# Three-pass fp32r products for values, queries and keys in a streaming attention, convolution and expert layer

## The reference, cut to what matters

```python
z = xn @ w_in                      # [c_q 512 | c_kv 512 | k_rope 64 | B 1024 | C 1024 | h 1024]
q = (rmsnorm(c_q, g_q) @ w_uq).reshape(B, T, N_HEADS, QK_NOPE + ROPE_DIM)   # 8 heads, 128 + 64
q_nope = q[..., :QK_NOPE]
q_rope = rope(q[..., QK_NOPE:], pos)
c_kv = rmsnorm(c_kv, g_kv)
k_rope = rope(k_r[:, :, None, :], pos)[:, :, 0, :]
q_lat = jnp.einsum('bthn,lhn->bthl', q_nope, w_uk)
...
o_lat = mla_attend(q_lat, q_rope, keys_ckv, keys_kr, pos, k_pos)
attn = jnp.einsum('bthl,lhv->bthv', o_lat, w_uv).reshape(B, T, ATTN_W)
...
conv_out = gate_b * conv           # short causal convolution over C * h
y = jnp.concatenate([rmsnorm(attn, g_ao), rmsnorm(conv_out, g_co)], axis=-1) @ w_o
```

## Time and profile before

| | |
|---|---|
| median of 3 runs | 1520.82 us (1520.22 to 1526.09) |
| the profiled execution's own time | 1520.34 us |
| its span, first to last instruction | 1518.4 us |
| TensorE busy, weight loads aside | 1343.2 us (88%) |
| VectorE busy | 590.5 us (39%) |
| ScalarE busy | 347.6 us (23%) |
| values, pairs of heads | 271 to 307 us, 307 to 419 us of the span |

### The profile page before, as it was taken

One profiled execution on the slowest core, in us unless ns is written; L12 is line 12 of the kernel. 1 busy time (PEld: TensorE's weight loads), 2 busy tenths in 40 slices (PEclk: granted clock), 3 DMA queues, 4 the chain that ended last, 5 costly groups with the idle time before them and its releaser, 6 DMA issues.

```text
span 1518.4 us, 22122 instructions
## 1 busy us (share of the span) xinstructions
PE 1343.2 (88%) x8510; PEld 714.2 (47%) x8511; DVE 590.5 (39%) x1175; ACT 347.6 (23%) x595; POOL 32.4 (2%) x41
## 2 busy tenths in 40 slices
PE   6999999999999999787888888888889988888885
PEld 4989999566666663232222222322323322232221
DVE  4335444044574443242243234224324422332344
ACT  5332322123453322111111111111212111111113
POOL 1000000000000000000000000000000000000000
PEclk9999999999999989999898888988989989898887
DMA  9454451023353368999999999999989999999994
GB/s 324 131 166 137 161 167 61 10 70 111 92 180 112 131 285 355 408 432 430 432 433 432 429 433 433 431 429 433 433 369 400 432 434 432 428 434 432 432 428 180
DMA packets 69751, 473.91 MB, mean 312 GB/s; under 512 B 9532, under 2 KB 46656, under 8 KB 55824
## 3 DMA queue, kind: packets, MB, share of 16 engines
q1 hardware_dynamic: 68640, 470.78, 76.0%
q0 software_dynamic: 832, 2.48, 0.4%
q10 hardware_dynamic: 240, 0.09, 0.0%
HBM read 469.97 MB, written 3.38 MB: 312 GB/s over the span
## 4 chain that ended last, share of the span: by engine, by line
PE 52%; DMA 41%; DVE 3%; issue 2%; ACT 1%; DVEq 0%; SPq 0%; ACTq 0%
DMA ring<-in_w_down 41%; PE ps L888 11%; PE ps L587 5%; PE ps L588 5%; PE ps L589 5%; PE ps L873 3%; PE ps L649 2%; PE ps L676 2%; PE ps L739 2%; PE ps L740 2%; PE ps L741 2%; PE ps L752 2%; PE ps L850 2%; PE ps L670 1%; PE ps L879 1%
## 5 line engine op out<-in xcount | busy, mean ns | idle before, releaser
L1566 DVE TENSOR_TENSOR hreg<-ps,hreg 128x512 f32<-128x512 f32 (+1 forms) x396 | 239.4, 677 | 291.6 <-PE ps L899 291.6
L873 PE MATMUL ps<-ring,mix 128*32 128x512 f32 x2112 | 278.4, 675 | 31.7 <-DMA ring<-in_w_up 19.5
L888 PE MATMUL ps<-ring,mix 128*32 128x512 f32 x1056 | 165.7, 784 | 62.5 <-DMA ring<-in_w_down 54.7
L899 PE MATMUL ps<-mix 32*128 32x512 f32 (+1 forms) x792 | 156.3, 612 | 26.4 <-ACT mix L1249 25.6
L1206 ACT COPY mix<-ps 128x512 f32<-128x512 f32 x66 | 70.5, 1068 | 446.4 <-PE ps L873 446.4
L873 PEld LDWEIGHTS ps<-ring,mix 128*32 128x32 f32 x2112 | 74.5, 121 | 206.3 <-issue 176.2
L587 PE MATMUL ps<-xT_hi,w_hi 128*128 128x320 f32 (+1 forms) x528 | 165.6, 314 | 2.9 <-DVE w_lo L1301 2.9
L588 PE MATMUL ps<-xT_lo,w_hi 128*128 128x320 f32 (+1 forms) x528 | 164.6, 312 | 0.0
L589 PE MATMUL ps<-xT_hi,w_lo 128*128 128x320 f32 (+1 forms) x528 | 164.5, 312 | 0.0
L1301 DVE TENSOR_TENSOR w_lo<-ring,w_hi 128x1024 fp32r<-128x1024 f32 (+1 forms) x66 | 76.8, 1204 | 110.5 <-ACT w_hi L1019 110.5
L888 PEld LDWEIGHTS ps<-ring,mix 128*32 128x32 f32 x1056 | 39.6, 138 | 162.7 <-issue 104.4
(11 more groups left out here) (258 smaller groups left out, 1186.5 us busy)
## 6 DMA issues: line engine op xcount, KB each, us to landing
ring<-in_w_gate SPq DMA_DIRECT2D x31, 4096.0 KB, 22.2
ring<-in_w_up SPq DMA_DIRECT2D x31, 4096.0 KB, 23.7
ring<-in_w_down SPq DMA_DIRECT2D x31, 4096.0 KB, 23.7
ring<-in_w_in SPq DMA_DIRECT2D x32, 1024.0 KB, 8.2
ring<-in_w_o SPq DMA_DIRECT2D x16, 1024.0 KB, 6.7
ring<-in_w_up SPq DMA_DIRECT2D x2, 2048.0 KB, 11.7
ring<-in_w_gate SPq DMA_DIRECT2D x2, 2048.0 KB, 8.4
ring<-in_w_down SPq DMA_DIRECT2D x2, 2048.0 KB, 22.3
```

Of the source, the lines that this page charges most:

```text
L873: last = pe.matmul(ps[r:r + B, bank, :], x[:, k % 4, k // 4, :], w[:, k, :], start=k < 4, stop=k >= KC - 4)
L888: last = pe.matmul(ps[B * j:B * (j + 1), 4, :], h[:, c, :], w[:, c, 512 * j:512 * j + 512], start=c == 0, stop=c == 3)
L899: pe.matmul(ps[0:tn, COMB_BANKS[u % 8], :], gates[r, t0:t0 + tn], rows[r, :], start=True, stop=True).then_inc(full_sem, 1)
L1566: dve.tensor_tensor(h, ps[0:tn, COMB_BANKS[u % 8], :], h, ALU.add).then_inc(signal, 1)
```

## The change

The products of values, queries and keys are each formed in three fp32r passes from high and low parts. ScalarE casts each operand to fp32r, VectorE subtracts the cast from the original. The operands are the four chunks of `wv` (128x1024 each), of `ckv` (128x576 each), `cq` (128x1280), and per pair of heads the rotary columns (128x512), the other columns of w_uq (128x1024) and w_uk (128x1024). The rotary columns of the two heads are laid side by side, so that their product is one with 128 columns of weights per chunk. The low parts of `wv`, `ckv`, `cq` and of the pairs' weights take the place of the originals; `rope_lo` has a place of its own. `wv_hi` lies in slot 3, and `wk_hi` (two pairs in turn) over its first half; most of `ckv_hi`, and `cq_hi` with `rope_lo`, lie in the second halves of slots 4 and 5.

```diff
+            pe.wait_ge(wv_lo_ready, LC)
...
                     for c in range(LC):
-                        last = pe.matmul(b[0:kn, :], ckv[:, c, k0:k0 + kn], wv[:, c, 512 * v:512 * v + 512], start=c == 0, stop=c == LC - 1)
+                        if k == v == 0:
+                            pe.wait_ge(ckv_lo_ready, c + 1)
+                        x_hi, x_lo = ckv_hi[c][:, k0:k0 + kn], ckv_lo[:, c, k0:k0 + kn]
+                        pe.matmul(b[0:kn, :], x_hi, wv_hi[:, c, f], start=c == 0, stop=False)
+                        pe.matmul(b[0:kn, :], x_hi, wv_lo[:, c, f], start=False, stop=False)
+                        last = pe.matmul(b[0:kn, :], x_lo, wv_hi[:, c, f], start=False, stop=c == LC - 1)
...
             def queries_and_keys(p):
-                wait_weights(W_PAIR + p)
+                pe.wait_ge(cq_lo_ready, 1)
+                pe.wait_ge(wq_lo_ready, 2 * p + 1)
                 b = claim(pe, f"qr{p}")
                 for c in range(LC):
-                    for i in range(2):
-                        last = pe.matmul(b[64 * i:64 * i + 64, 0:T], wq[:, c, QKD * i + NOPE:QKD * (i + 1)], cq[:, c, :],
-                                         start=c == 0, stop=c == LC - 1)
+                    pe.matmul(b[:, 0:T], rope_hi[p][:, c, :], cq_hi[:, c, :], start=c == 0, stop=False)
+                    pe.matmul(b[:, 0:T], rope_hi[p][:, c, :], cq_lo[:, c, :], start=False, stop=False)
+                    last = pe.matmul(b[:, 0:T], rope_lo[:, c, :], cq_hi[:, c, :], start=False, stop=c == LC - 1)
...
+                pe.wait_ge(wq_lo_ready, 2 * p + 2)        # q: the same three passes
...
+                pe.wait_ge(wk_lo_ready, p + 1)            # K: the same three passes
...
+            def values_hi(first, end):                     # ScalarE
+                act.wait_ge(slot_full[slot_of_item(W_UV)], slot_count(W_UV))
+                act.wait_ge(w_lo_ready, 2 * split_index[f"h{NCH - 1}"] + 2)
+                for c in range(first, end):
+                    act.copy(wv_hi[:, c, :], wv_raw[:, c, :]).then_inc(wv_hi_ready, 1)
+            def queries_hi(p):
+                act.wait_ge(slot_full[slot_of_item(W_PAIR + p)], slot_count(W_PAIR + p))
+                act.copy(rope_hi[p][:, :, :].rearrange("p c (i r) -> p c i r", i=2), wq_raw(p)[:, :, :, NOPE:QKD]).then_inc(wq_hi_ready, 1)
+                act.copy(wq_hi[p][:, :, :, :], wq_raw(p)[:, :, :, 0:NOPE]).then_inc(wq_hi_ready, 1)
+            def keys_hi(p):
+                act.wait_ge(psum_full, full(f"K{2 * p - 3}_1" if p >= 2 else "V4_1"))
+                act.copy(wk_hi[:, p % 2], wk_raw(p)).then_inc(wk_hi_ready, 1)
...
                 for name in "hB":
                     for i in range(2):
+                        if j == NCH // 2 - 1 and name == "h":
+                            values_hi(2 * i, 2 * i + 2)
                         split_hi(split_index[f"{name}{2 * j + i}"] + 2)
...
+            act.wait_ge(normed, 2 * LC)
+            act.wait_ge(psum_full, full(f"B{NCH - 2}"))
+            for c in range(LC):
+                act.copy(ckv_hi[c], ckv[:, c, :]).then_inc(ckv_hi_ready, 1)
+            act.copy(cq_hi[:, :, :], cq[:, :, :]).then_inc(cq_hi_ready, 1)
+            queries_hi(0)
             for k, (k0, kn) in enumerate(KT):              # copies of V
...
+            keys_hi(0)
             act.wait_ge(ssq_full, 3)
...
             queries(0)
+            queries_hi(1)
+            keys_hi(1)
             for p in range(H // 2):
                 exps(2 * p)
                 exps(2 * p + 1)
...
                 if p + 1 < H // 2:
                     queries(p + 1)
+                if p + 2 < H // 2:
+                    queries_hi(p + 2)
+                    keys_hi(p + 2)
                 mix_hi(NCH + 2 * p)
                 mix_hi(NCH + 2 * p + 1)
-                if p in (1, 2):
-                    w_o_hi(2 * p - 2, 2 * p)
+                if p == 1:
+                    w_o_hi(0, 2)
+                if p == 2:
+                    act.wait_ge(psum_full, full(f"K{H - 1}_1"))
+                    w_o_hi(2, 4)
...
+            # VectorE: values_lo, queries_lo, keys_lo subtract what values_hi, queries_hi, keys_hi cast
-                for c in (2 * j, 2 * j + 1):
+                for i, c in enumerate((2 * j, 2 * j + 1)):
+                    if j == NCH // 2 - 1:
+                        values_lo(2 * i, 2 * i + 2)
                     split_lo(split_index[f"h{c}"] + 2)
                     conv_input(c)
                 for c in (2 * j, 2 * j + 1):
                     split_lo(split_index[f"B{c}"] + 2)
+                    if c == NCH - 1:
+                        for m in range(LC):
+                            dve.wait_ge(ckv_hi_ready, m + 1)
+                            dve.tensor_tensor(ckv_lo[:, m, :], ckv[:, m, :], ckv_hi[m].bitcast(F32), ALU.subtract).then_inc(ckv_lo_ready, 1)
                     conv(c)
+            dve.wait_ge(cq_hi_ready, 1)
+            dve.tensor_tensor(cq_lo[:, :, :], cq[:, :, :], cq_hi[:, :, :].bitcast(F32), ALU.subtract).then_inc(cq_lo_ready, 1)
+            queries_lo(0)
...
+            keys_lo(0)
             scale_chunks(3, [mix[:, 8 + c, :] for c in range(NCH)], P_CO)
...
                         drain(name, dve.tensor_copy(kt[:, p % 2, i, k0:k0 + kn], bank(name)[:, 0:kn]))
+                        if i == 0 and s == 1 and p + 1 < H // 2:
+                            queries_lo(p + 1)
+                            keys_lo(p + 1)
```

More of the change, by code:

```diff
@@ L195, in trunk_layer_kernel @@
         m_lo = nc.alloc_sbuf_tensor_at("m_lo", [P, KC, T], F32R, offset=mix_at)
+        spare_at = parts_at - 4 * SLOT
+        half_slot = 4 * SLOT // 2
+        r2_at, ckv_at = hreg_at + 4 * 3 * D, mix_at + 4 * KC * T
+        wv_at = ring_at + 4 * SLOT * slot_of_item(W_UV)
+        wv_hi = nc.alloc_sbuf_tensor_at("wv_hi", [P, LC, NCH * VD], F32R, offset=spare_at)
+        wv_lo = nc.alloc_sbuf_tensor_at("wv_lo", [P, LC, NCH * VD], F32R, offset=wv_at)
+        ckv_hi_head = nc.alloc_sbuf_tensor_at("ckv_hi_head", [P, LC - 1, KEYS], F32R, offset=parts_at + half_slot)
+        ckv_hi_last = nc.alloc_sbuf_tensor_at("ckv_hi_last", [P, KEYS], F32R, offset=r2_at + 4 * 5184)
+        ckv_hi = [ckv_hi_head[:, c, :] for c in range(LC - 1)] + [ckv_hi_last[:, :]]
+        ckv_lo = nc.alloc_sbuf_tensor_at("ckv_lo", [P, LC, KEYS], F32R, offset=ckv_at)
+        cq_hi = nc.alloc_sbuf_tensor_at("cq_hi", [P, LC, T], F32R, offset=parts_at + 4 * SLOT + half_slot)
+        cq_lo = nc.alloc_sbuf_tensor_at("cq_lo", [P, LC, T], F32R, offset=ckv_at + 4 * LC * KEYS)
+        pair_at = [ring_at + 4 * SLOT * slot_of_item(W_PAIR + p) for p in range(H // 2)]
+        wq_lo = [nc.alloc_sbuf_tensor_at(f"wq_lo{p}", [P, LC, 2, QKD], F32R, offset=pair_at[p]) for p in range(H // 2)]
+        wk_lo = [nc.alloc_sbuf_tensor_at(f"wk_lo{p}", [P, LC, 2 * NOPE], F32R, offset=pair_at[p] + 4 * 1536) for p in range(H // 2)]
+        wq_hi = [nc.alloc_sbuf_tensor_at(f"wq_hi{p}", [P, LC, 2, NOPE], F32R, offset=pair_at[p] + 4 * 2560) for p in range(H // 2)]
+        rope_hi = [nc.alloc_sbuf_tensor_at(f"rope_hi{p}", [P, LC, 2 * ROPE], F32R, offset=pair_at[p] + 4 * 3584) for p in range(H // 2)]
+        rope_lo = nc.alloc_sbuf_tensor_at("rope_lo", [P, LC, 2 * ROPE], F32R, offset=parts_at + 4 * SLOT + half_slot + 4 * LC * T)
+        wk_hi = nc.alloc_sbuf_tensor_at("wk_hi", [P, 2, LC, 2 * NOPE], F32R, offset=spare_at)
         mflat = mix[:, :, :].rearrange("p c t -> p (c t)")
@@ L294, in trunk_layer_kernel @@
         drained = {"act": sem("drained_act"), "dve": sem("drained_dve")}
+        wv_hi_ready, wv_lo_ready = sem("wv_hi_ready"), sem("wv_lo_ready")
+        ckv_hi_ready, ckv_lo_ready = sem("ckv_hi_ready"), sem("ckv_lo_ready")
+        cq_hi_ready, cq_lo_ready = sem("cq_hi_ready"), sem("cq_lo_ready")
+        wq_hi_ready, wq_lo_ready = sem("wq_hi_ready"), sem("wq_lo_ready")
+        wk_hi_ready, wk_lo_ready = sem("wk_hi_ready"), sem("wk_lo_ready")
         s_ones, first_half = sem("s_ones"), sem("first_half")
@@ L366, in w_raw, with wq_raw, wk_raw @@
             return w[:, 8 * half:8 * half + 8, col:col + width]
+        wv_raw = wslot(W_UV).rearrange("p (c n) -> p c n", c=LC)
+        def wq_raw(p):
+            return wslot(W_PAIR + p)[:, 0:1536].rearrange("p (c i q) -> p c i q", c=LC, i=2)
+        def wk_raw(p):
+            return wslot(W_PAIR + p)[:, 1536:2560].rearrange("p (c n) -> p c n", c=LC)
         def o_raw(v):
@@ L647, in _ @@
                     b = claim(pe, f"V{k}_{v}")
+                    f = slice(512 * v, 512 * v + 512)
                     for c in range(LC):
-                        last = pe.matmul(b[0:kn, :], ckv[:, c, k0:k0 + kn], wv[:, c, 512 * v:512 * v + 512], start=c == 0, stop=c == LC - 1)
+                        if k == v == 0:
[4 more added lines that the diff above has]
+                        last = pe.matmul(b[0:kn, :], x_lo, wv_hi[:, c, f], start=False, stop=c == LC - 1)
                     last.then_inc(psum_full, 1)
```

(26 more changed lines are left out.)

6 lines of the change are left out of this document (removed).

## The result

The changed kernel takes 1511.42 us (median of 7, 1507.61 to 1515.14) against 1520.82 (7 runs, 1517.18 to 1526.09), a ratio of 0.9932 with the interval 0.9919 to 0.9944. It is faster by 0.7%, where 1503, 1.2%, was forecast. The profiled execution took 1507.61 us.

The account below looks back on a forecast made before the run. It took the edited part as bound by the columns TensorE streams: −18.3 us there plus 0.9 of stalls is −17.4, so 1520.3 becomes 1502.9, or 1503. The range was 1497 to 1510.

Parts of the forecast that it names:

- The passes: TensorE's new fp32r passes in values, queries and keys: 231, 147 and 119 ns for 512, 320 and 256 columns.
- Rival A: New TensorE passes run at their stream's pace, 216, 136 and 109 ns: −5.4 us more, 1497.5; chance 0.08.
- Rival B: 256-column passes take 147 ns (2.7 us) and rope columns the dear price (1.1 us): 1506.7; chance 0.10.
- The stall before attend: VectorE's three subtractions for the next pair delay attend by 0.4 us in each of two rounds: +0.9 us.
- The splits around B6: ScalarE and VectorE splitting work beside the late projections fits into their slack: cost 0.
- The sum for the edited part: Values, rotary, queries and keys on TensorE −18.3 us, plus 0.9 of stalls: −17.4 us net.
- the values: V product on TensorE: 120 passes of 231 ns, 27.7 us for 34.5, −6.8 us.
- the three later rounds: Attention rounds of pairs 1 to 3: 11.7 us per pair in place of 14.6, less 0.4 us stalls in two.
- Rival E: Splitting is served in line, TensorE waiting for all 39.1 us of it: slower, 1541; chance 0.02.
- After attention nothing is edited: Behind attention, expert loop included, the block shifts unchanged with its 29.14 us cadence, so the −17.4 us reaches the end.
- D: No change: the gain is made but the expert loop's transfers do not start earlier, 1520; chance 0.03.
- C: Late splits stall the pair rounds and V's start by two or three microseconds each: 1509 to 1512; chance 0.07.

Follow-up runs that it names:

- 32 increments: Both kernels with 32 semaphore increments added at the head of TensorE's program: changed kernel 1503.02 us, kernel before 1522.17 us.
- no branch: Both kernels without the count, branch and code for more than 32 tokens in TensorE's program for expert 0: changed 1500.26 us, before 1519.55 us.
- 128 increments: Both kernels with 128 semaphore increments added at the head of TensorE's program: changed 1512.16 us (1505.2 less the late head), before 1532.24 us (1524.9).
- 64 increments: Both kernels with 64 semaphore increments added at the head of TensorE's program: changed kernel 1501.67 us, kernel before 1517.73 us.
- 48: Changed kernel with 48 semaphore increments at TensorE's head and the next pair's subtractions moved behind the probability copies: 1502.62 us, ratio 0.9864.
- 192 increments: Changed kernel with 192 semaphore increments added at the head of TensorE's program: 1525.28 us, 1508.2 less the late head.

## Why the prediction was wrong

**Right, by the trace.** The passes: 512, 320 and 256 columns at the rows' own 231, 147 and 119 ns, where the 256 was drawn between two rows. From the first values to the first scores it is now 40.1 us (272.4 to 312.5). Rival A, passes at the stream's pace, fell: a 256-column pass takes 120 ns and not 109. Rival B fell, with 120 and not 147, and the strided rope columns at 0.60 us against my 0.64. The stall before attend: 0.4 us in two rounds, forecast and shown, and shown again by its removal (0.9 us). The splits around B6, at the start of the values and at the first keys cost nothing. The sum for the edited part, −17.4 us, is exact, with some luck: the values gave 0.7 us more than forecast and the three later rounds 0.6 less. Rival E, splitting served in line, is excluded by that sum.

**Wrong: the step "After attention nothing is edited. ... so the block shifts as it is, its 29.14 us cadence included."** The block did not shift as it is. Its cadence held: from the load that the first down product releases to the last it is 876.1 us before and 876.2 after. Its start held too: expert 0's first product begins 17.9 us earlier (569.84 and 551.96), where 17 was forecast. What failed lies between the two, in expert 0, whose time the prediction took as unchanged. 120 more matmuls and as many weight loads (the page's counts) moved TensorE's code behind them (30 packets of the instruction queue in the changed kernel, 29 before), and expert 0's wait for instructions went from 0.97 to 5.68 us. In the profiled execution that took 4.9 of the 17.9 us with which the gate of expert 1 was issued earlier, and as transfers pace everything behind, it was never won back. Nearly without that wait the changed kernel is 8.4 us faster (32 increments) and without it 11.2 (no branch), against the first measurement; against the repeat these are 5.3 and 8.0. Where both kernels have like waits, they are 19.2 us apart (32 increments), 19.3 (no branch) and 20.1 (128 increments), the 17.4 and a little more. With 64 increments, where neither stands before its first product, they are 16.1 apart, so this comparison is good to some 2 us and no better.

The Trainium skill has the rule, and I did not weigh it: "Runtime: NRT & Kernel Launch", Instruction fetch mechanics, says that instructions arrive in blocks of 16 KiB, and that a taken branch whose target is not in the current window of two blocks stalls the engine until that block arrives. The trace agrees in kind: the packets are of that size (30 are 0.49 MB), one starts 2.2 to 2.7 us before the end of every wait, and the wait before the first product goes when the branch goes. The waits within a product have no branch in them, and that rule does not cover them. Nor does the trace bear out a window of two: the first pass through the experts' loop brings three packets (582 to 610 us), and the 30 passes behind it, to the end of the span, none. In the changed kernel between 572 and 575 us, in which TensorE stands:

```profile
q8 instruction: 1, 0.02, 1.9%
```

That page gives no length. Here it is 0.9 to 6.7 us. In the wait of 5.68 us the DMA share was 1.02, so the weights' transfers took the DMA engines' whole time; whether they are what makes the packet late was not tested.

**None of the rivals was this one.** D held that the loop keeps its start; its first product moved by 17.9 us and its last load by 12.9. C put the loss into late splits; it would have given the same 1509 to 1512 for a reason that the trace excludes.

**Open.** Two measurements of the identical changed kernel gave 1511.42 and 1508.30, ratios of 0.9932 and 0.9908 whose intervals just overlap, with the same waits in both profiles to 0.2 us. These 3 us I can't assign. The medians of the first measurement are 9.4 us apart where the spans of the profiled executions are 12.9 apart (the changed kernel's was the fastest of its seven), so the 4.9 us account for the profile's distance and leave 3.5 us of the median's open; in the repeat the medians are 12.9 apart too (1521.19 and 1508.30). These 3 us decide whether the result lies inside 1497 to 1510; they do not change that 5 us of the gain went in expert 0. What decides when an instruction packet starts is open. How long a wait becomes at a given position was not predicted by anything here either: 32, 48, 64, 128 and 192 increments gave waits without an order that I could read.

## What to carry to other kernels

A forecast for one part of a long program should allow some microseconds for code that it only pushes along: look in the trace for an engine that stands with nothing to wait for behind a branch or in straight code, and for a packet of an instruction queue 2 to 3 us before it resumes, and treat those waits as part of the edit's price. When two kernels are compared, compare their unexplained waits first; a few instructions of padding at a place where the engine is idle tell whether a difference belongs to the edit or to the code's position. For the edit itself, the pace of a pass read from another stage of the same trace was good to 1%.

## What the runs showed of the hardware

- TensorE waited 0.9 to 6.7 us for instructions, behind a branch or in straight code (4.13 us between the 24th and the 25th matmul of a product). The length was the same within 0.2 us in two executions of one kernel, and changed with 32 more instructions hundreds of microseconds earlier.
- In all 22 such waits TensorE resumed 2.2 to 2.7 us after the start of a 16 KB packet of the instruction queue. The code of a loop came once, in its first pass, and 30 further passes brought no packet (changed kernel, 610 us to the end).
- Only the first of these waits reached the end: 4.78 us less of it gave 5.3 to 8.4 us, 5.1 us less of the second at most 1.4.
- Behind waits of 5.4 to 6.7 us TensorE's next product took 5.0 to 6.5 us, with a granted clock of 0.66 to 0.72 where it was read, and 3.64 us at 1.00 without one. Shorter waits went either way: 3.64 us behind 0.90, 0.94 and 1.01 us, but 5.24 behind 0.97, 5.18 behind 1.63 and 5.34 behind 2.36.
- A semaphore increment by TensorE takes 0.15 us.
- An fp32r pass takes 120, 147 and 231 ns for 256, 320 and 512 columns, 13 to 18 ns over the columns' own time at 2.4 GHz, whichever tensors it reads.
